# Attention outputs of a hybrid encoder layer copied and added in portions of four query tiles instead of two

## Chip, cores and metric

The kernel runs on one core of a Trainium2 chip. The metric is the device time of one execution in microseconds, as a median over runs; lower is better.

## The reference

One layer of an encoder on a stream of 1024 positions, model width 1024, all in float32: an RMS norm and an input projection; latent attention with 8 heads beside an RWKV-7 recurrence with 8 heads; an output projection; cross-attention to 256 memory tokens; a squared-ReLU MLP with 4096 hidden columns; a final norm. The change lies in the first attention. Cut to that:

```
s = (einsum('bqhd,bkhd->bhqk', qn, k_nope) + einsum('bqhr,bkr->bhqk', qr, k_rope)) * scale
s = where(key_chunk <= q_chunk, s, -inf)          # chunks of 64 positions
p = softmax(s, axis=-1)
o = einsum('bhqk,bkhd->bqhd', p, v)               # 64 value columns per head
o = rms_norm(o, out_norm)                         # per head
```

## The kernel before, in words

Everything is kept transposed, with features on the 128 partitions and the 1024 positions along the free dimension. Each engine has a program of its own, written out by hand, and the engines meet at semaphores. A class `Steps` names every step of a stage on an engine; a wait names the step that it needs, and the list of names (lines 440 to 461) must be in the order in which the engine issues them.

The attention stage runs over 8 heads h and, in each, over 8 query tiles q of 128 positions (here also called slots 0 to 7). A tile sees the keys 0 to 128(q + 1). The steps of a tile are:

- `s` (TensorE, L1071, with a mask product at L1074): the scores of tile q, into PSUM banks 0 to 3.
- `m` (VectorE, `row_max`, L2289): the negative row maximum.
- `e` (ScalarE, `mla_exp`, L1727): the exponential, PSUM to SBUF, with the row sums.
- `t` (TensorE, `mla_turn`, L1085): the probabilities transposed, into banks 4 and 5; `t` (ScalarE, `turned`, L1736) copies them to SBUF.
- `o` (TensorE, `mla_values`, L1102 and L1106): the product with the values, into bank 6. A head has 64 value columns, so the array's halves of 64 columns work on even and odd key tiles: the result of a tile is a sum of two halves of the partitions ("own" and "other").
- `oc` (ScalarE, `keep_other`, L1745) copies the other half from bank 6 to the own partitions of `mO` in SBUF, and then `o` (VectorE, `keep_o`, L2298) adds the own half of bank 6 to it. This is done for two query tiles at once, 256 columns: ScalarE and VectorE issue it in slots 3, 5 and 7 and at the end of the head. The value product of tile q then waits for the addition of the portion before its own (bank 6 is half used, columns 0 to 255 again and again).

TensorE issues in slot q: the scores of q, the turn of q - 1, the values of q - 2, then filler. The filler (`g_fill`, `g_half`, L970) is the input projection of later units, spread over heads 0 to 5 by a plan of quotas; the matmuls of half a unit go to bank 7 and are evicted by VectorE (`evict_half`, L2204 and L2208), in the slot in which the half ends. The next half's first matmul waits for this eviction. In VectorE's queue of a slot stand, in this order, the row maximum, the norm of the pair before in one slot, the addition `keep_o`, the eviction, and the preparation steps below. The query projection of the next head (L1030 to L1034) and the multiplication by the rotary table (`queries`, L2283) come at slot 7.

Heads 6 and 7 have no filler. Beside them go the steps `prep(0, s)` of the recurrence's first pair of heads, placed by `beside_heads(h, q)`: low-rank products (L1140), exponentials with changes of ScalarE's table (L1782 to L1793), elementwise work on VectorE (L2339 to L2402), the 64x64 blocks (L1187, L2387), which SP stores and reads back, and the inverse of their 16x16 blocks by a recurrence on VectorE (L2412, L2415) in slots 5, 6 and 7 and at the end of head 7. Its result is stored in DRAM by SP (L636, L637) and read back in another arrangement (L646); TensorE's first block product of the recurrence's loop (L1277) waits for these reads, and the reads wait also for the last value product.

After two heads GpSimd squares the pair's outputs (`pair_norm`, L779), once the last addition of the pair is done; TensorE sums the squares (L1114), and `o_out` (L2311) scales.

Of the kernel before, what the change touches and what calls it, by code (L numbers as in the profile page):

```python
# [12 lines left out]
ALU = mybir.AluOpType  # L13
AX_X = mybir.AxisListType.X

P = 128
# [148 lines left out]
def build(nc, x_t, mem_t, pos, wall, vecs, con_d, headw, wv_d, lora_d, out_t):  # L165
    with ExitStack() as ctx:
# [245 lines left out]
        for g in range(SLOT_END):  # L412
            n, part, j = part_of(g)
# [27 lines left out]
        for h in range(MLA_HEADS):  # L441
            p, last = h // 2 - 1, h == MLA_HEADS - 1
            for q in range(NW):
                m_pe += [f"s{h}_{q}"] + [f"t{h}_{q - 1}"] * (q >= 1) + [f"o{h}_{q - 2}"] * (q >= 2)
                m_act += [f"e{h}_{q}"] + [f"t{h}_{q - 1}"] * (q >= 1) + [f"oc{h}_{q // 2 - 1}"] * (q in (3, 5, 7))
                m_dve += [f"m{h}_{q}"]
                if p >= 0 and h % 2:
                    m_pe += [f"sp{p}_0", f"sp{p}_1"] * (q == 0)
                    m_dve += [f"ot{p}_0", f"ot{p}_1"] * (q == 1)
                m_dve += [f"o{h}_{q // 2 - 1}"] * (q in (3, 5, 7))  # L450
                if p >= 0 and h % 2 == 0:
                    m_pe += [f"sm{p}"] * (q == 1)
                    m_dve += [f"s2{p}", f"vr{p}"] * (q == 1)
            m_pe += [f"qp{h + 1}"] * (not last) + [f"t{h}_7"] + [f"kp{h + 1}"] * (not last) + [f"o{h}_6", f"o{h}_7"]
            m_pe += [f"vp{h // 2 + 1}"] * (h % 2 == 1 and not last)
            m_act += [f"t{h}_7"] + [f"k{h + 1}"] * (not last) + [f"oc{h}_3"] + [f"v{h // 2 + 1}"] * (h % 2 == 1 and not last)
            m_dve += [f"q{h + 1}"] * (not last) + [f"o{h}_3"]
            m_pool += [f"sq{h // 2}", f"pw{h // 2}"] * (h % 2 == 1)
        p = PAIRS - 1
        m_dve += [f"s2{p}", f"vr{p}", f"ot{p}_0", f"ot{p}_1"]  # L460
# [291 lines left out]
        def _(pool):  # L752
# [20 lines left out]

            def pair_norm(p):

                pool.wait_ge(M_DVE.sem, M_DVE.at(f"o{2 * p + 1}_3", -1))
                if p >= 1:
                    pool.wait_ge(o_stored, 16 * p)
                nc.gpsimd.tensor_tensor(o_stage[:, :], mO[p % 2], mO[p % 2], ALU.mult).then_inc(M_POOL.sem, M_POOL.one(f"sq{p}"))  # L779
                pool.wait_ge(M_DVE.sem, M_DVE.at(f"vr{p}", -1))  # L780
                nc.gpsimd.tensor_tensor(mFac, mSq, con[:, C_NH:C_NH + 16], ALU.pow).then_inc(
                    M_POOL.sem, M_POOL.one(f"pw{p}"))
# [122 lines left out]
        def _(pe):  # L905
# [110 lines left out]
            def m_at(st, name):  # L1016
                pe.wait_ge(st.sem, st.at(name, -1))
# [70 lines left out]
            def mla_values(h, q):  # L1088

                m_at(M_ACT, f"t{h}_{q}")  # L1090
                j, hd = q // 2, h % 2
                if j >= 1:
                    m_at(M_DVE, f"o{h}_{j - 1}")
                elif h >= 1:
                    m_at(M_DVE, f"o{h - 1}_3")
                else:
                    pe.wait_ge(half_free, FILL - 4)
                own, other = (slice(HD * n, HD * n + HD) for n in (hd, 1 - hd))
                at = slice(P * (q % 2), P * (q % 2) + P)
                if q == 0:  # L1100
                    for rows, cols in ((slice(0, HD), own), (slice(HD, P), other)):
                        last = nc.tensor.matmul(PS[cols, 6, at], mV[rows, 0, HD * hd:HD * hd + HD], mPT[0][rows, 0:P],  # L1102
                                                start=True, stop=True)
                else:
                    for k in range(q + 1):
                        last = nc.tensor.matmul(PS[own if k % 2 == 0 else other, 6, at], mV[:, k, HD * hd:HD * hd + HD],  # L1106
                                                mPT[q % 2][:, win(k)], start=(k < 2), stop=(k >= q - 1))
                last.then_inc(M_PE.sem, M_PE.one(f"o{h}_{q}"))
# [542 lines left out]
        def _(act):  # L1651
# [55 lines left out]
            def m_at(st, name):  # L1707
                act.wait_ge(st.sem, st.at(name, -1))
# [28 lines left out]
                    M_ACT.sem, M_ACT.one(f"t{h}_{q}"))  # L1737

            def keep_other(h, j):
                hd, n = h % 2, 2 * P  # L1740
                own, other = (slice(HD * k, HD * k + HD) for k in (hd, 1 - hd))
                m_at(M_PE, f"o{h}_{2 * j + 1}")
                if j == 0 and hd == 0 and h >= 4:
                    m_at(M_DVE, f"ot{h // 2 - 2}_1")
                nc.scalar.copy(mO[h // 2 % 2][own, n * j:n * j + n], PS[other, 6, 0:n]).then_inc(  # L1745
                    M_ACT.sem, M_ACT.one(f"oc{h}_{j}"))
# [172 lines left out]
            for h in range(MLA_HEADS):  # L1919
                if h % 2 == 0 and h >= 4:  # L1920
                    m_at(M_DVE, f"vr{h // 2 - 2}")
                for q in range(NW):
                    mla_exp(h, q)
                    if q >= 1:
                        turned(h, q - 1)
                    if q in (3, 5, 7):
                        keep_other(h, q // 2 - 1)
                    for s in beside_heads(h, q):
                        prep(0, s)
                turned(h, NW - 1)  # L1930
                for s in beside_heads(h, NW):
                    prep(0, s)
                if h < MLA_HEADS - 1:
                    keys(h + 1)
                keep_other(h, 3)
                if h % 2 == 1 and h < MLA_HEADS - 1:
                    values(h // 2 + 1)

# [203 lines left out]
        def _(dve):  # L2142
# [132 lines left out]
            def m(ins, name):  # L2275
                ins.then_inc(M_DVE.sem, M_DVE.one(name))

            def m_at(st, name):
                dve.wait_ge(st.sem, st.at(name, -1))
# [10 lines left out]
                                          negate=True), f"m{h}_{q}")  # L2290

            def keep_o(h, j):
                hd, n = h % 2, 2 * P
                own = slice(HD * hd, HD * hd + HD)
                m_at(M_PE, f"o{h}_{2 * j + 1}")
                m_at(M_ACT, f"oc{h}_{j}")
                o = mO[h // 2 % 2][own, n * j:n * j + n]
                m(nc.vector.tensor_tensor(o, PS[own, 6, 0:n], o, ALU.add), f"o{h}_{j}")  # L2298

            def pair_sums(p):  # L2300
                m_at(M_ACT, f"e{2 * p + 1}_{NW - 1}")
# [212 lines left out]
            for h in range(MLA_HEADS):  # L2514
                for q in range(NW):
                    row_max(h, q)
                    p = h // 2 - 1
                    if h % 2 == 1 and h >= 3 and q == 1:
                        o_out(p, 0)
                        o_out(p, 1)  # L2520
                    if q in (3, 5, 7):
                        keep_o(h, q // 2 - 1)
                    if h % 2 == 0 and h >= 2 and q == 1:
                        pair_sums(p)
                    if q < NW - 1:
                        filled(h, q)
                        for s in beside_heads(h, q):
                            prep(0, s)
# [8 lines left out]
                        evict_half(u, half)  # L2537
                for s in beside_heads(h, NW):
                    prep(0, s)
                keep_o(h, 3)  # L2540
            def attention_end(s):
                if s == 2:
                    pair_sums(PAIRS - 1)
# [435 lines left out]
```

## Time and profile before

| | us |
|---|---|
| median of 3 runs | 1856.16 |
| the runs | 1856.16, 1854.52, 1862.93 |
| the profiled execution | 1852.6 |
| its span, first to last instruction | 1850.5 |

| engine | busy, us | share |
|---|---|---|
| TensorE | 1741.0 | 94% |
| VectorE | 992.4 | 54% |
| ScalarE | 793.5 | 43% |
| GpSimd | 703.9 | 38% |

The mean granted clock of TensorE in the profiled execution is 0.97 of the full level (2.4 GHz). A row of the timeline gives the start in us from the span's beginning, the duration in us, the engine, the line, the operation with output and inputs, and in brackets how long the engine had been idle before it and whose work ended that. PE is TensorE, DVE is VectorE, ACT is ScalarE, POOL is GpSimd; PEld is TensorE's weight load. In rows by stage the order is TensorE, its weight loads, VectorE, ScalarE, GpSimd (busy us and instructions), then the granted clock, DMA share and GB/s.

### The profile page before, as it was taken

The page shows a single profiled execution, that of the slowest core. Times are in us where ns is not written, and L with a number is a line of the kernel's source. Part 1 is how long each engine was busy: PE and PEld are TensorE (multiplying, and loading weights), DVE is VectorE, ACT ScalarE, POOL GpSimd, SP SyncE. Part 2 cuts the span into 40 slices and gives each one's busy share as a digit, 9 for nine tenths or more (in the row PEclk, how much of TensorE's full clock was granted, in tenths as well). Part 3 has the DMA queues.
Part 4 walks back from the last instruction along what each step waited for, and adds up shares of the span by engine and source line. Part 5 has one row for each costly group of instructions (what it writes and reads, how often), then busy time and mean ns, then how long its engine had stood idle before and what let it go on. Part 6 is the DMA issues. An engine that isn't in the chain of part 4 may idle for free.

```text
span 1850.5 us, 29970 instructions
## 1 busy us (share of the span) xinstructions
PE 1741.0 (94%) x11908; PEld 1332.4 (72%) x11908; DVE 992.4 (54%) x1549; ACT 793.5 (43%) x1530; POOL 703.9 (38%) x505
## 2 busy tenths in 40 slices
PE   4999999998788889899999999999999999999996
PEld 3766666655566666668898768778888888888885
DVE  6542232335464655463350262378856775884787
ACT  4313332244233343452130231367566666766762
POOL 1220211011120211232242202297695876968761
PEclk9999999988689999999999999999999999999998
DMA  5101010001111112242211101212112022020202
GB/s 195 53 24 32 23 34 10 21 5 29 41 19 42 20 43 42 88 145 87 88 41 51 34 1 34 76 50 69 50 42 92 23 69 67 26 92 23 69 1 91
DMA packets 81681, 94.35 MB, mean 51 GB/s; under 512 B 53648, under 2 KB 56208, under 8 KB 81552
## 3 DMA queue, kind: packets, MB, share of 16 engines
q1 hardware_dynamic: 81552, 92.56, 15.9%
q8 instruction: 89, 1.46, 0.3%
q14 instruction: 40, 0.33, 0.1%
HBM read 82.57 MB, written 9.98 MB: 50 GB/s over the span
## 4 chain that ended last, share of the span: by engine, by line
PE 84%; DVE 8%; issue 3%; ACT 2%; DMA 1%; POOL 1%; SPq 0%; DVEq 0%; ACTq 0%; POOLq 0%
PE PS L1615 32%; PE PS L922 16%; PE PS L970 8%; PE PS L1071 3%; PE PS L1106 2%; PE PS L1085 2%; PE PS L1140 2%; PE PS L1562 1%; PE PS L1541 1%; PE PS L1433 1%; PE PS L1143 1%; PE PS L1335 1%; PE PS L1418 1%; PE PS L1277 1%; PE PS L1030 1%
## 5 line engine op out<-in xcount | busy, mean ns | idle before, releaser
L1615 PE MATMUL PS<-memr,wsp 128*128 128x512 f32 x1332 | 321.2, 392 | 0.9 <-POOL wsp L883 0.9
L922 PE MATMUL PS<-xn,wsp 128*128 128x512 f32 x1344 | 309.6, 392 | 6.7 <-DVE xn L2158 6.7
L922 PEld LDWEIGHTS PS<-xn,wsp 128*128 128x128 f32 x1344 | 253.5, 189 | 62.0 <-DVE xn L2158 5.0
L1615 PEld LDWEIGHTS PS<-memr,wsp 128*128 128x128 f32 x1332 | 250.6, 188 | 56.0 <-POOL wsp L883 1.3
L762 POOL CAST wsp<-wraw 128x1024 fp32r<-128x1024 f32 x40 | 43.4, 1085 | 472.9 <-PE PS L922 306.5
L1615 PE MATMUL PS<-memr,wraw_r 128*128 128x512 f32 x684 | 167.7, 394 | 5.4 <-DVE memr L2721 3.3
L1615 PEld LDWEIGHTS PS<-memr,wraw_r 128*128 128x128 f32 x684 | 129.0, 189 | 35.2 <-DVE memr L2721 3.7
L970 PE MATMUL PS<-xn,wsp 128*128 128x512 f32 x576 | 146.7, 401 | 3.2 <-DVE proj L2208 3.1
L883 POOL TENSOR_TENSOR wsp<-sa,wsp 128x512 fp32r<-128x512 f32 x86 | 115.1, 1340 | 81.0 <-ACT wsp L2047 80.9
L970 PEld LDWEIGHTS PS<-xn,wsp 128*128 128x128 f32 x576 | 104.4, 188 | 40.1 <-issue 20.2
L2721 DVE TENSOR_TENSOR memr<-PS,memr 128x512 fp32r<-128x512 f32 x168 | 114.6, 682 | 27.4 <-ACT PS L2068 27.4
L1727 ACT ACTIVATE H<-PS,mst 128x128 f32<-128x128 f32 (+3 forms) x64 | 47.5, 741 | 179.8 <-DVE mst L2289 178.2
L1615 PE MATMUL PS<-tmp_r,wsp 128*128 128x512 f32 x444 | 116.9, 397 | 0.0
L2739 DVE TENSOR_TENSOR H<-PS,H 128x512 f32<-128x512 f32 x128 | 86.7, 688 | 46.7 <-PE PS L1615 30.1
L2289 DVE TENSOR_REDUCE mst<-PS 128x1 f32<-128x128 f32 (+3 forms) x64 | 48.2, 754 | 117.3 <-PE PS L1074 117.3
L2063 ACT CAST memr<-sa 128x512 fp32r<-128x512 f32 x96 | 59.2, 617 | 95.1 <-PE PS L1615 78.6
L1615 PEld LDWEIGHTS PS<-tmp_r,wsp 128*128 128x128 f32 x444 | 83.4, 188 | 21.2 <-DVE tmp_r L2721 1.3
L764 POOL TENSOR_TENSOR wsp<-wraw,wsp 128x1024 fp32r<-128x1024 f32 x40 | 96.4, 2410 | 3.2
L867 POOL TENSOR_TENSOR sbx<-sa,sbx 128x512 f32<-128x512 f32 x64 | 85.9, 1342 | 4.7
L883 POOL TENSOR_TENSOR wsp<-sbx,wsp 128x512 fp32r<-128x512 f32 x62 | 82.9, 1341 | 11.1 <-ACT wsp L2047 11.0
L847 POOL TENSOR_TENSOR ssum<-con,rsm 64x256 f32<-64x256 f32 x32 | 27.3, 871 | 139.5 <-DVE ssum L2582 139.5
L1071 PE MATMUL PS<-H 128*128 128x512 f32 (+2 forms) x192 | 77.2, 512 | 0.0
(336 smaller groups left out, 3157.4 us busy)
## 6 DMA issues: line engine op xcount, KB each, us to landing
wraw<-in_weights_dram SPq DMA_DIRECT2D x40, 512.0 KB, 3.6
sa<-in_weights_dram SPq DMA_DIRECT2D x32, 512.0 KB, 4.3
H<-in_x_dram SPq DMA_DIRECT2D x16, 512.0 KB, 6.5
sbx<-in_weights_dram SPq DMA_DIRECT2D x32, 256.0 KB, 2.6
sa<-in_weights_dram SPq DMA_DIRECT2D x32, 256.0 KB, 2.6
H<-in_weights_dram SPq DMA_DIRECT2D x8, 512.0 KB, 6.7
out_dram<-sbx SPq DMA_DIRECT2D x16, 256.0 KB, 2.1
a_dram<-H SPq DMA_DIRECT2D x16, 128.0 KB, 2.5
```

The source lines that it names most:

```text
L764: nc.gpsimd.tensor_tensor(wsp[:, k, :, 1, :], raw, wsp[:, k, :, 0, :].bitcast(F32), ALU.subtract).then_inc(w_split, 1)
L867: nc.gpsimd.tensor_tensor(out, a, b, op).then_inc(W_SUM.sem, W_SUM.one(name))
L883: nc.gpsimd.tensor_tensor(w[:, 1, :], w_source(g), w[:, 0, :].bitcast(F32), ALU.subtract).then_inc(mw_rest, 1)
L922: last = nc.tensor.matmul(PS[:, 2 * k + half, :], wsp[:, k, kt, a, :], src[:, at, b, HALF * half:HALF * half + HALF], start=(i == 0 and (a ...
L970: last = nc.tensor.matmul(PS[:, bank, :], wsp[:, u % 2, kt, a, :], xn[:, kt, b, HALF * half:HALF * half + HALF], start=(kt == 0 and (a, b) ...
L1071: nc.tensor.matmul(PS[:, b + part, 0:n], mQ[:, win(q)], mK[:, HALF * part:HALF * part + n], start=True, stop=(part < q // 4))
L1615: last = nc.tensor.matmul(PS[:, g % PS_BANKS, :], w[:, a, win(k)], x[:, b, :], start=(k == 0 and (a, b) == (0, 0)), stop=(k == ROWS - 1 an ...
L1727: nc.scalar.activation(mP[q % 2][:, 0:n], two(2 * (q % 2))[:, 0:n], ACT.Exp, bias=mNeg[hd][:, q:q + 1], accum_out=mSum[h // 2 % 2][:, c:c ...
L2063: nc.scalar.copy(x_split_of(d)[:, 0, :], x_source(d)).then_inc(mx_head, 1)
L2289: m(nc.vector.tensor_reduce(mNeg[h % 2][:, q:q + 1], two(2 * (q % 2))[:, 0:P * (q + 1)], AX_X, ALU.max, negate=True), f"m{h}_{q}")
L2721: nc.vector.tensor_tensor(x[:, 1, :], PS[:, PS_BANKS + d % 2, :], x[:, 0, :].bitcast(F32), ALU.subtract).then_inc(mx_rest, 1)
L2739: out(nc.vector.tensor_tensor(tile, a, b, ALU.add), f"{kind}{part}_{v}")
```

## The change

The portion copied from and added out of bank 6 becomes four query tiles, 512 columns, the whole bank, instead of two tiles and half the bank. ScalarE and VectorE issue the pair in slot 5 and at the end of the head only. The value product of tile 4 waits for the first portion's addition, that of tile 0 for the second portion of the head before. The additions' steps are renamed from `o` to `a`. Nothing else is edited.

```diff
@@ lists of steps
-                m_act += [f"e{h}_{q}"] + [f"t{h}_{q - 1}"] * (q >= 1) + [f"oc{h}_{q // 2 - 1}"] * (q in (3, 5, 7))
+                m_act += [f"e{h}_{q}"] + [f"t{h}_{q - 1}"] * (q >= 1) + [f"oc{h}_0"] * (q == 5)
...
-                m_dve += [f"o{h}_{q // 2 - 1}"] * (q in (3, 5, 7))
+                m_dve += [f"a{h}_0"] * (q == 5)
...
@@ pair_norm, GpSimd
-                pool.wait_ge(M_DVE.sem, M_DVE.at(f"o{2 * p + 1}_3", -1))
+                pool.wait_ge(M_DVE.sem, M_DVE.at(f"a{2 * p + 1}_1", -1))
@@ mla_values, TensorE
-                j, hd = q // 2, h % 2
+                j, hd = q // 4, h % 2
                 if j >= 1:
-                    m_at(M_DVE, f"o{h}_{j - 1}")
+                    m_at(M_DVE, f"a{h}_{j - 1}")
                 elif h >= 1:
-                    m_at(M_DVE, f"o{h - 1}_3")
+                    m_at(M_DVE, f"a{h - 1}_1")
...
-                at = slice(P * (q % 2), P * (q % 2) + P)
+                at = slice(P * (q % 4), P * (q % 4) + P)
@@ keep_other, ScalarE
-                hd, n = h % 2, 2 * P
+                hd, n = h % 2, 4 * P
...
-                m_at(M_PE, f"o{h}_{2 * j + 1}")
+                m_at(M_PE, f"o{h}_{4 * j + 3}")
@@ the loop over slots, ScalarE
-                    if q in (3, 5, 7):
-                        keep_other(h, q // 2 - 1)
+                    if q == 5:
+                        keep_other(h, 0)
...
-                keep_other(h, 3)
+                keep_other(h, 1)
@@ keep_o, VectorE
-                hd, n = h % 2, 2 * P
+                hd, n = h % 2, 4 * P
...
-                m_at(M_PE, f"o{h}_{2 * j + 1}")
+                m_at(M_PE, f"o{h}_{4 * j + 3}")
                 m_at(M_ACT, f"oc{h}_{j}")
                 o = mO[h // 2 % 2][own, n * j:n * j + n]
-                m(nc.vector.tensor_tensor(o, PS[own, 6, 0:n], o, ALU.add), f"o{h}_{j}")
+                m(nc.vector.tensor_tensor(o, PS[own, 6, 0:n], o, ALU.add), f"a{h}_{j}")
@@ the loop over slots, VectorE
-                    if q in (3, 5, 7):
-                        keep_o(h, q // 2 - 1)
+                    if q == 5:
+                        keep_o(h, 0)
...
-                keep_o(h, 3)
+                keep_o(h, 1)
```

## Rows read from the trace of the kernel before

**Rows 1.** The page: busy time, share of the span and instructions.

```profile
PE 1741.0 (94%) x11908; PEld 1332.4 (72%) x11908; DVE 992.4 (54%) x1549; ACT 793.5 (43%) x1530; POOL 703.9 (38%) x505
```

**Rows 2.** Busy time by stretch, columns as told above.

```profile
120.00:390.00 270.00, 266.78 (x1505) 179.02 (x1505) 83.72 (x124) 82.72 (x179) 36.83 (x20) 1.00 0.06 21
390.00:474.00 84.00, 73.07 (x473) 41.34 (x469) 41.08 (x80) 40.45 (x77) 11.42 (x5) 0.86 0.08 19
399.00:412.00 13.00, 11.28 (x21) 3.64 (x21) 3.87 (x4) 6.42 (x9) 1.77 (x1) 0.50 0.00 0
478.00:511.00 33.00, 28.80 (x265) 20.31 (x266) 8.15 (x19) 8.03 (x17) 4.37 (x3) 0.50 0.20 50
```

**Rows 3.** Groups by shape: busy us, mean ns, idle before and releaser.

```profile
L2298 DVE TENSOR_TENSOR H<-PS,H 64x256 f32<-64x256 f32 x16 | 6.8, 422 | 44.9 <-ACT H L1745 44.9
L2298 DVE TENSOR_TENSOR mO_odd<-PS,mO_odd 64x256 f32<-64x256 f32 x16 | 6.7, 422 | 32.1 <-ACT mO_odd L1745 32.1
L1745 ACT COPY H<-PS 64x256 f32<-64x256 f32 x16 | 5.9, 366 | 9.4 <-PE PS L1106 9.2
```

**Rows 4.** A copy of 64x512 (duration min/median/max in ns), an addition of 128x512.

```profile
L1712 ACT COPY H<-PS x8: 578/580/581, 114.5 to 432.4; 64x512 f32<-64x512 f32 x8
...
L2739 DVE TENSOR_TENSOR H<-PS,H 128x512 f32<-128x512 f32 x128 | 86.7, 688 | 46.7 <-PE PS L1615 30.1 <-ACT con L2083 8.2 <-issue 7.2
```

**Rows 5.** Timeline, head 2, slots 5 and 6.

```profile
232.23 0.37 ACT L1745 COPY mO_odd<-PS 64x256 f32<-64x256 f32 x1
232.70 0.42 DVE L2298 TENSOR_TENSOR mO_odd<-PS,mO_odd 64x256 f32<-64x256 f32 x1 [2.10 <-ACT mO_odd L1745]
...
233.81 0.75 DVE L2208 SCALAR_TENSOR_TENSOR proj<-PS,vec,proj 128x511 f32<-128x511 f32 x1
...
234.70 1.62 PE L970 MATMUL PS<-xn,wsp 128*128 128x512 f32 x6 [0.15 <-DVE proj L2208]
```

**Rows 6.** Timeline, head 1, slots 3 and 4.

```profile
175.48 0.43 DVE L2298 TENSOR_TENSOR H<-PS,H 64x256 f32<-64x256 f32 x1 [1.67 <-ACT H L1745]
...
177.62 1.61 PE L970 MATMUL PS<-xn,wsp 128*128 128x512 f32 x6 [0.42 <-DVE proj L2208]
```

**Rows 7.** Timeline, head 6: slot 3, and its end.

```profile
413.34 0.37 ACT L1745 COPY mO_odd<-PS 64x256 f32<-64x256 f32 x1
...
436.13 0.41 DVE L2298 TENSOR_TENSOR mO_odd<-PS,mO_odd 64x256 f32<-64x256 f32 x1
```

**Rows 8.** Timeline, head 7, slot 3.

```profile
450.29 1.12 PE L1143 MATMUL PS<-proj,con 128*128 128x512 f32 x2
...
451.30 0.43 DVE L2298 TENSOR_TENSOR mO_odd<-PS,mO_odd 64x256 f32<-64x256 f32 x1 [1.67 <-ACT mO_odd L1745]
...
452.30 0.69 DVE L2402 TENSOR_TENSOR proj<-PS,proj 128x512 f32<-128x512 f32 x1
```

**Rows 9.** Timeline, head 7, VectorE in slots 5 and 7.

```profile
461.26 0.43 DVE L2298 TENSOR_TENSOR mO_odd<-PS,mO_odd 64x256 f32<-64x256 f32 x1 [2.10 <-ACT mO_odd L1745]
...
466.49 1.22 DVE L2289 TENSOR_REDUCE mst<-PS 128x1 f32<-128x1024 f32 x1
...
470.23 0.43 DVE L2298 TENSOR_TENSOR mO_odd<-PS,mO_odd 64x256 f32<-64x256 f32 x1 [2.52 <-ACT mO_odd L1745]
470.69 0.23 DVE L2412 TENSOR_TENSOR sc_s<-sc_s 128x63 f32<-128x63 f32 x1
```

**Rows 10.** Timeline, from the last value product and the recurrence's result to the first block product.

```profile
473.19 0.36 ACT L1745 COPY mO_odd<-PS 64x256 f32<-64x256 f32 x1 [1.19 <-PE PS L1106]
...
474.05 0.38 DVE L2418 COPY sc_s<-sc_s 128x256 f32<-128x256 f32 x1
...
478.95 1.28 SPq L646 DMA_DIRECT2D H<-x_dram  x2
...
479.42 0.69 PE L1260 MATMUL PS<-sc_s,sc_w 64*64 64x64 f32 x8 [0.18 <-ACT sc_s L1829]
...
484.13 1.12 PE L1277 MATMUL PS<-H 64*64 64x64 f32 x16 [4.02 <-DMA H<-xt_dram]
```

More of the change, by code:

```diff
@@ L455, in build @@
             m_pe += [f"vp{h // 2 + 1}"] * (h % 2 == 1 and not last)
-            m_act += [f"t{h}_7"] + [f"k{h + 1}"] * (not last) + [f"oc{h}_3"] + [f"v{h // 2 + 1}"] * (h % 2 == 1 and not last)
-            m_dve += [f"q{h + 1}"] * (not last) + [f"o{h}_3"]
+            m_act += [f"t{h}_7"] + [f"k{h + 1}"] * (not last) + [f"oc{h}_1"] + [f"v{h // 2 + 1}"] * (h % 2 == 1 and not last)
+            m_dve += [f"q{h + 1}"] * (not last) + [f"a{h}_1"]
             m_pool += [f"sq{h // 2}", f"pw{h // 2}"] * (h % 2 == 1)
```

## Prediction, made before the changed kernel was run

> **What bounds the kernel now.** The first view is the page: TensorE is busy for 94% of the span, no other engine for more than 54% [rows 1], so a step counts only where TensorE waits for it. The second view is busy time by stage. In the heads whose slots are filled with projection matmuls (120 to 390 us, nearly all of heads 0 to 5) TensorE is busy 266.78 of 270 us; in heads 6 and 7 (390 to 474 us), which have no such filler, 73.07 of 84 us, at a mean clock of 0.86 [rows 2]. So heads 0 to 5 can give back 3.2 us at most, whatever is taken from ScalarE and VectorE, and the question is heads 6 and 7. The third view, groups of instructions by shape, shows the edited pair: 32 copies of 64x256 at 366 ns on ScalarE and 32 additions at 422 ns on VectorE, and 44.9 + 32.1 = 77 us in which VectorE stood idle before an addition until the copy was done [rows 3]. That number is large because VectorE works strictly in order; it costs time only where the work queued behind the addition is itself waited for. The rest of the reading is a hunt for those places.
>
> **What changes.** 16 pairs of copy and addition in place of 32, each twice as wide, at query slot 5 and at the head's end instead of slots 3, 5, 7 and the end. TensorE's matmuls and their order stay. Each value product still waits once, for the addition that frees bank 6: o4 waits for the first portion, o0 of the next head for the second; the waits of o2 and o6 fall on work long done.
>
> **Prices.** A 64x512 copy out of PSUM stands in the trace: 580 ns. A 64x512 addition does not; its bounds are the 64x256 one (422 ns) and two of those (844 ns), and the addition over 128x512, as many elements per partition, takes 688 ns [rows 3, 4]. I take 690 ns, the nearest in shape. Per pair that is +0.21 us on ScalarE and +0.27 us on VectorE where a pair stays, and all of it away where one goes. Over the kernel ScalarE saves 32 x 0.366 - 16 x 0.580 = 2.4 us and VectorE 32 x 0.422 - 16 x 0.690 = 2.5 us, on engines that are about half idle.
>
> The Trainium skill (VectorE: DVE Perf Modes, the section on the TRN2 errata) says that each instruction pays a fixed cost once and advises tiles of 512 elements or more. Read as advice on the whole time it would credit the change with those 4.9 us; the stage view says that nearly all of them lie beside a busy TensorE.
>
> **Heads 0 to 5.** Two places matter, both evictions of the projection, which stand behind the addition in VectorE's queue and free the bank that the next filler wants. In head 2, slot 5, copy (232.23), addition (232.70) and eviction (ends 234.56) come in a row, and the filler at 234.70 already waits 0.15 us for it [rows 5]. The wider pair delays this by 0.21 + 0.27 = 0.48 us. Head 5 repeats the pattern (filler at 374.51): +0.96 us together. The opposite is found in heads 1 and 4, slot 3: there the pair disappears, the eviction can start when its matmuls end, about a microsecond earlier, and the filler's waits of 0.42 and 0.29 us go (head 1 is shown) [rows 6]: -0.71 us. Sum +0.25 us; ends +0.96 and -0.71. SP's and POOL's queues wait on these evictions only through the weight tiles, and POOL is idle for most of this stretch; hiding the rest is TensorE's own filler. If that cover were gone these heads would look like 6 and 7.
>
> **Head 6.** ScalarE is the chain from 412 to 421 us (two table loads, exponentials, copies). The copy at 413.34 goes: -0.39 us with its gap. At slot 5 the wider copy and addition stand between t4's copy and the next row maximum: +0.48 us. Net +0.1 us. At the head's end the addition at 436.13 sits in an unbroken run of VectorE work that TensorE waits for: +0.27 us [rows 7]. The addition removed at slot 7 was followed by a wait for the query projection, so it gives nothing.
>
> **Head 7, slot 3.** After the row maximum (ends 449.6) VectorE waited 1.67 us for the copy, added (451.30), wrote two small memsets and only then did the multiplication at 452.30 whose operand TensorE had finished at 451.42; the next score matmuls are behind that multiplication [rows 8]. Without the pair the memsets run early and it starts at 451.5: -0.79 us.
>
> **Head 7, slot 5.** Copy and addition stay, wider, with the block-inverse recurrence queued behind them: +0.48 us [rows 9].
>
> **Head 7, slot 7.** This is the largest term. The row maximum ends at 467.71. The addition then waits for the copy, which stands behind an exponential and a turned copy on ScalarE: 2.52 us idle, done at 470.66, and only at 470.69 does VectorE go on with the recurrence [rows 9], whose result (474.4) is stored, read back and waited for by TensorE until 484.13 [rows 10]. Without this portion the recurrence goes on at 467.71: -2.98 us. Is another wait hidden beneath? The reads of the stored blocks also wait for the last value product, done at 473.1 [rows 10], and for the stores, which would now land near 476; they then start at 476, still later. TensorE's work before the reads ends near 480.1 with the copies that follow it [rows 10]; the wider last addition, since VectorE now waits for its copy, moves this by -0.3 us, to 479.8, against 481.2 for the data. So 1.4 us of room remain and all 2.98 us pass. The store of the last pair and POOL's squaring behind the last addition start about 0.3 us earlier too, and the squares are first used after the reads.
>
> **Sum.** +0.25 + 0.1 + 0.27 - 0.79 + 0.48 - 2.98 = -2.67 us. By the ends of the addition's price (422 or 844 ns) the five wide additions in these chains change it by about -1.3 or +0.8 us. Against the profiled execution (1852.6 us, of it a span of 1850.5) that gives 1849.9 us. The median of the three runs stands 3.6 us above that execution; so I forecast 1856.2 - 2.7 = 1853.5 us. The three runs spread over 8.4 us, three times the effect, and about 0.5% (9 us) is what a measurement of this kernel can tell from no change.
>
> **Rivals.**
> First, nothing is gained: the early recurrence meets something the trace of before cannot show, such as the stores running slower beside other traffic, or the recurrence's interleaving with the row maxima shifting so that TensorE waits for those instead. It needs 1.4 us or more of new delay at 476 to 484 us to eat half the gain. Against it speaks that the DMA queue is otherwise empty there. Time: 1856.2 us.
>
> Second, TensorE's clock. It is granted at half level (1.2 GHz) from 478 to 511 us, TensorE busy 28.8 of 33 us [rows 2], right after a stretch of thin work and a 4 us idle gap before 484.13 [rows 10]. The change shortens that gap to about 1.4 us. If the full level survived it, up to half of 28.8 = 14.4 us would go; part of it is held by other engines, so I take 8: 1845.5 us. Against: the clock had fallen by 478, before the gap, in a stretch whose matmuls the change moves by only 0.3 to 0.6 us. The Trainium skill (TensorE: Matmul & The Clock Gate, on oscillation) says that idle gaps throttle the array and sustained work releases it; by that rule the shorter gap speaks for this rival, while the trace puts the fall ahead of the gap.
>
> Third, the other sign: one more half-level stretch in heads 6 and 7. There TensorE is idle in places, and the clock has already gone to half at 399 to 412 us with 11.28 us busy [rows 2]. If the delays at slot 5 thin out its work enough that the clock falls once more for as long, the loss is up to half of 11.28 = 5.6 us; with the gain, +2.9: 1859.1 us. It decides from a fall longer than about 6 us. The place to see it is 460 to 475 us, where the trace now grants the full clock. Slower by over 0.5% needs two such stretches.
>
> That the change does not do what it says is excluded by the code: each engine's list of steps and its waits are changed alike.
>
> **Chances.** Forecast 0.67; nothing gained 0.12; clock better 0.08; clock worse 0.13. The range 1846.0 to 1860.0 takes in the forecast with the addition's bounds, nothing gained, most of the clock cases and the spread of the runs. Faster by over 0.5% (under 1846.9) needs the clock case and a good draw: 0.05. Slower by over 0.5% (above 1865.4) needs two worse stretches or a disturbed set: 0.04. Within 0.5%: 0.91.
>
> **What would show each step.** The copy 16 times at 580 ns and the addition 16 times near 690; VectorE's idle before it falling from 77 us to about half; the fillers of heads 2 and 5 after slot 5 waiting 0.6 to 0.8 us, those of heads 1 and 4 not at all; no gap of 2.5 us on VectorE after the last row maximum of head 7; the first block matmul about 2.7 us earlier relative to the start. I am wrong if that matmul moves by less than 1 us or if heads 0 to 5 end over 1 us later.

## The result, and the profile after

| | before | after |
|---|---|---|
| median of 11 executions each, in alternation | 1856.16 us | 1846.1 us |
| ratio after/before, 95% interval | | 0.9938, 0.9915 to 0.996 |
| profiled execution | 1852.6 us | 1841.3 us |
| its span, mean granted clock | 1850.5 us, 0.970 | 1839.5 us, 0.972 |

The kernel became faster by 0.6% (0.4 to 0.85%), 10 us between the medians and 11.5 us by the ratio, where 2.7 us were forecast. One execution of the 11 after took 2455 us at a mean clock of 0.648, and in the runs further down one of e1 took 9312 us and one of e7 1865.3 us; the ratios leave these out.

**The edited pair** came out as priced. The groups by shape of the kernel after (busy us, mean ns, idle before and releaser):

```profile
L2298 DVE TENSOR_TENSOR H<-PS,H 64x512 f32<-64x512 f32 x8 | 5.5, 688 | 29.8 <-ACT H L1745 29.8
L2298 DVE TENSOR_TENSOR mO_odd<-PS,mO_odd 64x512 f32<-64x512 f32 x8 | 5.5, 688 | 20.7 <-ACT mO_odd L1745 20.7
L1745 ACT COPY H<-PS 64x512 f32<-64x512 f32 x8 | 4.6, 580 | 9.3 <-PE PS L1106 9.2
```

Against [rows 3], half the instructions, 688 ns (690 assumed) and 580 ns each. VectorE's idle time before them fell from 77 to 50.5 us, to two thirds where about half was expected. That fall of 26.5 us is not what the kernel gained: TensorE, as before, sets the time.

**The stages** (busy time by stretch; columns as in [rows 2]):

```profile
120.00:390.00 270.00, 266.61 (x1511) 179.12 (x1510) 82.03 (x112) 80.69 (x167) 36.82 (x20) 1.00 0.07 21
390.00:474.00 84.00, 73.45 (x442) 42.26 (x440) 40.15 (x77) 39.48 (x72) 11.41 (x5) 0.82 0.10 20
399.00:412.00 13.00, 10.63 (x17) 3.35 (x17) 3.45 (x3) 6.58 (x10) 1.58 (x1) 0.50 0.00 0
478.00:511.00 33.00, 31.32 (x480) 22.99 (x480) 17.82 (x39) 16.19 (x37) 6.26 (x5) 0.95 0.18 45
```

Heads 0 to 5 are as they were. The last row is the news. Before, 33 us at clock 0.50 held 265 matmuls [rows 2]; now they hold 480, at 0.95. TensorE reads as busy in both. A busy share says nothing of the pace: the count of matmuls and the clock column do.

The same work, cut at the same two instructions (from the first block product to the first state product of the recurrence), in the kernel after and then, in the second fence, before:

```profile
481.60:498.40 16.80, 16.41 (x260) 11.24 (x256) 8.32 (x15) 6.64 (x11) 4.49 (x3) 1.00 0.17 45
```

```profile
484.10:512.60 28.50, 28.47 (x250) 19.52 (x250) 7.94 (x15) 6.46 (x10) 4.37 (x3) 0.51 0.13 34
```

By the starts of those two instructions it is 28.51 - 16.74 = 11.8 us, as much as the whole difference of the two profiled executions (11.3 us). The first block product comes 2.5 us earlier than before, and the time after the first state product is 3.2 us longer (1839.5 - 498.4 against 1850.5 - 512.6). That last part was not followed further: two profiled executions of the unchanged kernel differ by 6.4 us (1852.6 and, in the first run below, 1859.0). The 2.5 us are one draw too: 0.9 of them stand already at the first key projection of the attention (113.42 against 112.55 us), and a second stretch at half level, near 440 us, which the prediction did not name, lasted about 10 us before and 7 us after.

**The place.** The timeline of the kernel after, head 7 slot 7 to the first block product:

```profile
466.03 1.22 DVE L2289 TENSOR_REDUCE mst<-PS 128x1 f32<-128x1024 f32 x1
...
467.16 0.22 DVE L2412 TENSOR_TENSOR sc_s<-sc_s 128x63 f32<-128x63 f32 x1
...
470.51 0.38 DVE L2418 COPY sc_s<-sc_s 128x256 f32<-128x256 f32 x1
...
475.43 1.28 SPq L646 DMA_DIRECT2D H<-x_dram  x2
...
481.36 0.45 PE L1260 MATMUL PS<-sc_s,sc_w 64*64 64x64 f32 x8 [0.18 <-ACT sc_s L1829]
...
481.64 0.63 PE L1277 MATMUL PS<-H 64*64 64x64 f32 x16
```

The 2.52 us stall of [rows 9] is gone, the recurrence goes on right behind the row maximum, and the read of the stored blocks is issued at 475.43 instead of 478.95 [rows 10]. TensorE no longer waits before the first block product: 4.02 us had been forecast to become 1.4, and became none. Why none? TensorE's own work ran later than forecast. Busy time by stretch, after:

```profile
466.00:470.00 4.00, 2.57 (x22) 2.06 (x23) 3.62 (x14) 2.01 (x4) 0.00 (x0) 0.69 0.01 4
470.00:474.00 4.00, 4.00 (x33) 3.67 (x33) 0.79 (x4) 1.01 (x1) 0.00 (x0) 0.50 0.48 57
474.00:478.00 4.00, 1.84 (x40) 1.19 (x37) 1.76 (x3) 0.58 (x1) 1.76 (x1) 0.93 0.27 51
478.00:482.00 4.00, 3.62 (x39) 3.25 (x41) 2.21 (x6) 1.75 (x8) 0.14 (x1) 0.60 0.85 192
482.00:486.00 4.00, 3.84 (x74) 3.55 (x70) 1.48 (x5) 0.12 (x1) 0.00 (x0) 1.00 0.59 163
```

and before:

```profile
470.00:474.00 4.00, 3.57 (x54) 2.75 (x53) 3.29 (x15) 1.50 (x3) 0.00 (x0) 1.00 0.00 0
474.00:478.00 4.00, 1.68 (x25) 1.47 (x26) 3.13 (x6) 0.31 (x2) 1.89 (x1) 0.95 0.56 66
478.00:482.00 4.00, 1.94 (x19) 1.33 (x18) 0.95 (x5) 1.56 (x7) 0.00 (x0) 0.50 0.29 66
482.00:486.00 4.00, 1.87 (x30) 1.75 (x32) 0.58 (x2) 0.00 (x0) 0.00 (x0) 0.50 0.98 202
```

After, TensorE's clock fell to half already in 466 to 474 us, came back, fell once more, and was full from 482 on. Before, it fell at about 478 and stayed at half through the wait and the step behind it. The early fall stretched TensorE's own work so far that the data were there when it asked. The Trainium skill (TensorE: Matmul & The Clock Gate, on what is actually happening and on oscillation) has activity release the throttle and idle gaps bring it back. These two traces fit the second half: thin work and gaps stand ahead of each of these falls. The first half does not hold for the step before, busy 28.47 of 28.5 us and not raised. That step is made of small products in the main, but not of those alone: 9.6 us of it are products of 512 columns (L1140 and L1143).

### The profile page after: what moved, and what is told of

Its sections match the earlier page's. It is cut to its first block, busy times and chain, and to the rows that moved or that the text cites. A ratio compares the mean times of both kernels' runs of the same rounds, so it can differ in the third digit from the quotient of the medians.

```text
span 1839.5 us, 29922 instructions
## 1 busy us (share of the span) xinstructions
PE 1735.1 (94%) x11908; PEld 1330.3 (72%) x11908; DVE 992.0 (54%) x1533; ACT 791.1 (43%) x1514; POOL 703.9 (38%) x505
## 4 chain that ended last, share of the span: by engine, by line
PE 84%; DVE 8%; issue 2%; ACT 2%; DMA 1%; POOL 1%; SPq 1%; DVEq 0%; ACTq 0%; POOLq 0%
PE PS L1615 32%; PE PS L922 16%; PE PS L970 8%; PE PS L1071 3%; PE PS L1106 2%; PE PS L1085 2%; PE PS L1562 2%; PE PS L1140 1%; PE PS L1541 1%; PE PS L1433 1%; PE PS L1143 1%; PE PS L1335 1%; PE PS L1418 1%; PE PS L1030 1%; PE PS L1366 1%
```

## The experiments

Each kernel ran in alternation with the kernel before, whose median was 1859.0 us beside e1 to e4, 1856.7 beside e5 to e8 and 1857.3 beside e9 to e12; these three sets ran on three chips. Here is what they gave; the texts on record and what follows from each come after. "Wait" is TensorE's idle time ahead of the first block product in the profiled execution, "step" the time from it to the first state product, with its clock; the last column counts executions under 1848 us, which is below every one of the 115 of the kernel before in all sets (lowest 1850.3). It is no exact measure of the level in the step: the profiled execution of e10 had the full level there and took 1849.5 us.

| label | median us | ratio to before (95%) | wait | step (clock) | under 1848 |
|---|---|---|---|---|---|
| before, first set | 1856.2 | | 4.0 | 28.5 (0.51) | 0 of 11 |
| after | 1846.1 | 0.9938 (0.9915-0.996) | none | 16.8 (1.00) | 7 of 11 |
| e1_before_again | 1857.9 | 0.9988 (0.9965-1.0011) | 4.8 | 28.8 (0.51) | 0 of 12 |
| e2_after_again | 1846.1 | 0.9936 (0.991-0.9963) | none | 16.8 (1.00) | 7 of 12 |
| e3_late_four | 1858.9 | 0.9985 (0.9954-1.0015) | 2.2 | 28.5 (0.52) | 2 of 12 |
| e4_stall_back | 1854.8 | 0.9974 (0.9948-1.0001) | 1.1 | 29.0 (0.51) | 0 of 12 |
| e5_before_gap | 1849.0 | 0.9973 (0.995-0.9996) | filled, 0.5 left | 16.8 (1.00) | 5 of 12 |
| e6_after_busy | 1851.6 | 0.9968 (0.9954-0.9983) | 2.3 | 28.6 (0.52) | 2 of 12 |
| e7_head7_four | 1844.2 | 0.9926 (0.9904-0.9949) | 2.3 | 28.5 (0.52) | 7 of 11 |
| e8_early_four | 1857.4 | 1.001 (0.9988-1.0033) | 2.6 | 28.6 (0.52) | 0 of 12 |
| e9_heads05_four | 1857.0 | 1.0005 (0.9984-1.0026) | 3.2 | 28.9 (0.51) | 0 of 12 |
| e10_head7_gap | 1852.7 | 0.9979 (0.9957-1.0) | filled | 16.8 (1.00) | 4 of 12 |
| e11_head7_gap_scores | 1845.5 | 0.9938 (0.9913-0.9963) | filled | 23.9 (0.64) | 9 of 12 |
| e12_head7_four_again | 1846.2 | 0.9961 (0.9934-0.9987) | none | 16.7 (1.00) | 7 of 12 |

**Both kernels again**, unchanged, as a measure of chance.

> The kernel before, once more, for a second profile of it. Theory A (the earlier block data keep TensorE's clock up in the recurrence's loop): the ratio to the kernel before is 1.000 within 0.2%, and in this profile too the clock is at half level from about 478 us to past 505 us. Theory B (where the clock falls and rises is chance in each execution, and the two profiles compared were two draws): the stretch at half level after 478 us differs by 10 us or more from that of the first profile.

> The changed kernel, once more. Theory A: ratio about 0.994 again, and the clock is at the full level from about 482 us on in this profile as well. Theory B: about 0.9985 (the 2.7 us of the sum) with a clock stretch of any length.

The kernel before came out at 1857.9 us with the same half-level step behind a wait of 4.81 us; the kernel after at the same median as the first time. So 0.6% is the change's and no draw of one set. One part of the first expectation missed: the level was not at half from 478 us on but full until about 485, and fell within the wait (483.0 to 487.8 us):

```profile
478.00:482.00 4.00, 1.93 (x28) 1.53 (x28) 3.12 (x7) 0.81 (x5) 1.89 (x1) 1.00 0.56 66
482.00:486.00 4.00, 0.85 (x16) 0.57 (x16) 0.53 (x2) 0.98 (x5) 0.00 (x0) 0.92 0.41 94
```

So in one and the same program the level falls ahead of the wait or within it, and the step is slow either way. In e2 the first block product came at 487.21 us, only 0.6 us earlier than in e1 and 5.6 us later than in the first profile of the same kernel. Its half-level stretch near 440 us lasted 17 us, where those of before and e1 lasted 10 and that of after 7:

```profile
448.00:452.00 4.00, 3.54 (x21) 1.85 (x22) 1.05 (x3) 0.00 (x0) 0.00 (x0) 0.50 0.15 31
452.00:456.00 4.00, 3.22 (x10) 0.98 (x8) 1.51 (x4) 1.15 (x3) 0.00 (x0) 0.50 0.62 98
```

Yet TensorE had no wait and the step took 16.8 us, at full level from 487 us on and not, as theory A had it, from 482. That the block product comes early is not what makes the step quick.

**Other portions.** The bounds of the portions were made a function of the head, which all loops, waits and step lists read; the kernels differ in its one line. Its versions, one under the other:

```
return ((0, 2), (2, 4), (4, 8))                                            # e3_late_four
return ((0, 4), (4, 6), (6, 8))                                            # e8_early_four
return ((0, 4), (4, 8)) if h == 7 else ((0, 2), (2, 4), (4, 6), (6, 8))    # e7, e12
return ((0, 4), (4, 8)) if h < 6 else ((0, 2), (2, 4), (4, 6), (6, 8))     # e9
```

The first, e3, keeps two-tile portions early and has no addition in slot 7, so the stall of [rows 9] is gone in it.

> Portions of 2, 2 and 4 tiles: the pair of slot 7 goes, those of slots 3 and 5 stay as before. Theory A: this carries nearly the whole gain, since the recurrence's result is stored about 3 us earlier: the first block product starts near 481 us, the clock is up from about 482 us, ratio 0.993 to 0.995. Theory B: the first block product is early by 3 us but the ratio is 0.998.

The wait shrank to 2.19 us, and the step ran at half level; 0.9985 is no difference that can be told. Theory A had the block product near 481 us and a ratio of 0.993 to 0.995, and missed with both; theory B's ratio came, its block product 3 us early did not:

```profile
485.52 0.68 PE L1295 MATMUL PS<-H 64*64 64x64 f32 x16 [2.19 <-DMA H<-xt_dram]
```

This speaks against the reading that the removed stall alone buys 10 us. In this profile the level was full through the wait and fell within the first microsecond of the step.

**The stall put back.** The change as it is, but VectorE waits in head 7, slot 7, for ScalarE's turned copy, where the removed addition had held it.

```diff
                     if q == 5:
                         keep_o(h, 0)
+                    if h == MLA_HEADS - 1 and q == NW - 1:
+                        m_at(M_ACT, f"t{h}_{q - 1}")
```

> The changed kernel with one wait added: in head 7, slot 7, VectorE waits after the row maximum for ScalarE's turned copy of tile 6, about 2.3 us. Theory A: the data come 2.3 us later than in the changed kernel, the clock stays at half level after 484 us as before, and most of the 10 us are lost again: ratio 0.998 to 1.000. Theory B: 2.3 us slower than the changed kernel and no more.

The stall returned at 2.06 us, TensorE waited 1.11 us, and the median is 8.7 us above that of the change:

```profile
468.67 1.22 DVE L2289 TENSOR_REDUCE mst<-PS 128x1 f32<-128x1024 f32 x1
...
471.96 0.23 DVE L2412 TENSOR_TENSOR sc_s<-sc_s 128x63 f32<-128x63 f32 x1 [2.06 <-ACT H L1736]
...
485.67 1.12 PE L1277 MATMUL PS<-H 64*64 64x64 f32 x16 [1.11 <-DMA H<-xt_dram]
```

Two microseconds of stall cost over eight, and none of the twelve executions came under 1848 us. The level fell at about 480 us, ahead of the wait, as it had after (478 us); after, without a wait, it rose at 481, and here, behind 1.1 us of wait, it stayed at half through the step. So the stall is needed for the slower outcome here, though, by e3, its absence is not enough for the quicker one.

**The wait filled.** Two full 128x512 products whose results nobody reads, between TensorE's last wait ahead of the block products and the first of these, in the kernel before.

```diff
+            def keep_busy(n):
+                r_at(P_DVE, "bv1_0")
+                for _ in range(n):
+                    nc.tensor.matmul(PS[:, 7, :], ident, con[:, 0:HALF], start=True, stop=True)
...
             pe.wait_ge(rp_dve, RP_SET)
+            keep_busy(2)
```

> The kernel before, portions of two, with two 128x512 products of constants into the free bank 7 where TensorE waits 4 us for the block data. Nothing is computed from them. Theory A (it is TensorE's wait ahead of the loop that keeps the clock at half level to 513 us): the clock is up within a few us of 484 us, and 8 us or more are gained with the portions unchanged, ratio 0.994 to 0.997. Theory B (chance, or the portions themselves): ratio 1.000 and the half level lasts to past 505 us.

```profile
479.60 3.78 PE L1441 MATMUL PS<-con 128*128 128x512 f32 x4
...
483.88 0.70 PE L1277 MATMUL PS<-H 64*64 64x64 f32 x16 [0.50 <-DMA H<-xt_dram]
```

Here nothing of the portions was changed and the stored blocks are as late as ever. The level fell at about 477 us, as in the first profile of before, and came back at 484.0, as the first block product started; there it had stayed down past 511 us. The step ran at full level, 16.8 us, in the profiled execution, the median is 7.7 us below that of the kernel before beside it, and 5 of 12 executions came under 1848 us, where the kernel before never does. The ratio, 0.9973, is just short of what theory A asked for. So it is the idle wait on TensorE, and not the data's lateness, that goes with the slow step in this pair. It is the cleanest of the experiments, and it also shows that filling the wait is no sure cure. The filling is itself work of 512 columns; that other work, or none but an absent wait, does as well is shown by the kernel after.

**More filling.** The change with such products elsewhere in thin places: two in slot 7 of head 7, one before the last turn, one behind each of the first two score steps, and none in the wait.

> The changed kernel with such products in five places where TensorE waits: two in slot 7 of head 7, one before its last turn, one behind each of the first two score steps of the loop. Theory A: the clock stays at the full level through 466 to 482 us and the low executions of the changed kernel vanish; ratio 0.990 to 0.993. Theory B: each product costs up to its 0.9 us, ratio 0.994 to 0.996 and the same spread.

A half-level step in the profiled execution, behind a wait of 2.26 us, only 2 of 12 under 1848 us, and 0.9968, slower than either theory's ratio. The level itself was full from 466 to 482 us, as theory A had it, and through the wait; it fell within the first microsecond of the step. So a level held up to the wait was no help here. The products' own time is in the 1851.6 us.

**Which heads.** Next came the change in head 7 alone (e7), in heads 0 to 5 alone (e9), and the early four (e8), which keeps an addition in slot 7.

> Portions of four in head 7 alone, two elsewhere. Theory A: the whole direct gain of 3 us (slots 3 and 7 of head 7) plus the clock, so ratio 0.993 to 0.995 with heads 0 to 6 unchanged. Theory B: ratio 0.998.

> Portions of 4, 2 and 2 tiles: the pair of slot 3 goes, those of slot 7 and the end stay as before. Theory A: the direct gain is under 1 us, the data come as late as before and the clock stays low: ratio 0.999 to 1.000. Theory B (the whole effect hangs on how the work falls, from anywhere): any ratio from 0.994 to 1.003.

> Portions of four in heads 0 to 5 only, two in heads 6 and 7. By the sum heads 0 to 5 lose about 0.25 us and everything behind them stays: ratio 1.000 within 0.2%, clock at half level from 478 to past 505 us in nearly every execution. If the wider portions there mattered, the ratio would lie outside 0.998 to 1.002.

Head 7 alone gives as much as the whole change (0.9926, and 0.9961 the second time), heads 0 to 5 nothing (1.0005), and the early four, whose addition in slot 7 still waits for its copy, nothing (1.001):

```profile
475.83 0.43 DVE L2318 TENSOR_TENSOR mO_odd<-PS,mO_odd 64x256 f32<-64x256 f32 x1 [2.53 <-ACT mO_odd L1764]
```

The profiled execution of e7 is one of the four of eleven that took longer (1853.2 us). It shows a full level ahead of the wait and a half-level step behind it:

```profile
478.00:482.00 4.00, 1.71 (x24) 1.24 (x22) 1.56 (x5) 1.79 (x8) 0.00 (x0) 1.00 0.74 168
...
482.43 0.78 PE L1295 MATMUL PS<-H 64*64 64x64 f32 x16 [2.30 <-DMA H<-xt_dram]
...
482.40:510.90 28.50, 28.41 (x252) 19.27 (x252) 7.94 (x15) 6.47 (x10) 4.38 (x3) 0.52 0.11 31
```

**The same kernel once more** (e12), with e10 and e11, which add products in the wait, and in the wait and behind each score step, to head 7 alone.

> Portions of four in head 7 alone, once more, for a second profile and more executions. Ratio 0.992 to 0.995 again. Theory A: where the profiled execution is a fast one (under 1845 us), the first state product follows the first block product by about 17 us; where it is a slow one, by about 28 us.

> Portions of four in head 7 alone, and two 128x512 products of constants into the free bank 7 where TensorE waits 2.3 us for the block data. Theory A (TensorE's wait there decides the clock of the loop's first step): nearly all executions have the full level from the first block product on, so the first state product follows it by 17 and not by 28 us; ratio 0.990 to 0.992. Rival (the portions' gain is used up, the products only cost): ratio 0.993 to 0.995 and the spread stays.

> As the kernel before this one, with one more such product behind each of the first two score steps, where TensorE waits 1.6 and 0.8 us. If more filling keeps the clock up more often: ratio 0.988 to 0.991. If these products delay the block product instead (the 0.8 us wait is shorter than the product): 1 us slower than the kernel with the two products alone.

This time the profile caught one of the quick executions of that kernel:

```profile
483.22 0.63 PE L1295 MATMUL PS<-H 64*64 64x64 f32 x16
...
483.20:499.90 16.70, 16.31 (x258) 11.20 (x252) 8.32 (x15) 6.64 (x11) 4.49 (x3) 1.00 0.16 45
```

e7 and e12 are one program. With a wait of 2.30 us the step took 28.5 us, with none 16.7: 11.8 us, and the twelve executions of e12 lie in two groups, 7 between 1843 and 1848 us (mean clock 0.971 to 0.974) and 5 between 1855 and 1861 us (0.963 to 0.966), about 12 us apart. The program does not decide which of the two an execution takes, and the share differs from kernel to kernel. That the two groups are the two outcomes of this step is inferred from the distance and the clock; one execution of e12 was profiled.

e11 has the most executions in the quick group (9 of 12) and no better median, and its profile shows the step at full level for about five microseconds only, though TensorE had not waited ahead of it:

```profile
485.70:489.70 4.00, 3.84 (x71) 3.62 (x72) 1.37 (x4) 0.00 (x0) 0.00 (x0) 1.00 0.36 121
489.70:507.00 17.30, 17.30 (x168) 10.45 (x164) 5.00 (x9) 5.19 (x10) 4.04 (x3) 0.54 0.01 2
```

e10 went the other way than hoped, 4 of 12 and a median of 1852.7 us, slower than either theory had it. Filling the wait lets the level be full in the profiles (e5, e10 and, for a while, e11), while over all executions it helps the kernel before (0 of 115 to 5 of 12) and does nothing that can be told for head 7 alone (7 of 11 and 7 of 12, against 4 and 9 of 12).

**What the profiles say together.** Of 14 (before, after and the twelve), eight have an unfilled wait, of 1.1 to 4.8 us: the step took 28.5 to 29.0 us in all eight. In the six without one it began at full level, and took 16.7 to 16.8 us in five.

The wait is not the whole of it. In e3, e6, e7 and e8 the level was still full when the block product started behind a wait of 2.2 to 2.6 us, and fell within the first microsecond of the step. In e11, whose wait was filled and whose level had been full since 477 us, it fell at about 491. All five quick steps came the other way: the level had fallen less than ten microseconds before the block product and rose within a microsecond of its start, or in e10 2.5 us before it. There are five more profiles in which it had fallen in those ten microseconds, all with a wait (before, e1, e4, e9, and e8, where it had come back at 487.2 us, 2.9 us ahead of the block product, and was lost again), and in all of them the step ran at half level. So in these ten the wait tells the two outcomes apart. Where the level had not fallen in that time (e3, e6, e7, e11), no profile shows it held, with a wait or without; whether the removal of the wait is worth anything there is not shown.

**The rest, with the clock taken out.** Each execution comes with its mean granted clock. A line through the executions of one kernel, time against clock, read at 0.967, gives 1857.4 us for the kernel before beside e1 to e4, one execution at a clock of 0.921 left out (1856.6 and 1857.5 in the two later sets), 1855.1 and 1853.2 for the change (e2), 1853.9 and 1854.0 for head 7 alone, 1854.4 for the late four, 1855.4 for the early four, 1856.6 for heads 0 to 5. At one clock the change is worth 2.3 us (4.2 in e2), head 7 alone 2.7 and 3.5, the late four about 3, heads 0 to 5 about 1 or nothing. These are fits through a dozen points each, good to perhaps a microsecond or two. They would suit a direct part of the size of the forecast sum, 2.7 us, in head 7, but they don't show it: the same line gives 1854.9 us for e4, 2.5 us under the kernel before, though its stall is back.

The timelines say a little more. From head 6's first low-rank product (L1140) to the first block product it is 90.9 us in before and 91.8 in e1, 89.0 in after and 92.8 in e2, 87.7 and 88.4 with head 7 alone (e7, e12), and 93.2 in e9. Where the half-level stretch near 440 us is equally long, 10 us, head 7 alone has the block product 2.5 to 4.1 us earlier (before and e1 against e7 and e12); where it lasts 17 us, the change has it 0.4 us earlier (e2 against e9).

## Why the prediction was wrong, by its own steps

The sum of the direct effects has its size confirmed only within a microsecond or two; the step that failed is the weighing of the second rival, which put the clock behind the wait at 0.08 and at nothing in the sum.

- **Prices**: copy 580 ns, addition 688 ns (690 taken). Right.
- **Heads 0 to 5**, +0.25 us: from the first key projection to the first low-rank product behind head 5 it is 279.8 us before and 280.0 after. The fillers of heads 2 and 5 wait 0.60 and 0.73 us (0.63 and 0.77 by the sum); those of heads 1 and 4 don't wait. Head 2, from the timeline after:

```profile
230.94 0.58 ACT L1745 COPY mO_odd<-PS 64x512 f32<-64x512 f32 x1
231.62 0.68 DVE L2298 TENSOR_TENSOR mO_odd<-PS,mO_odd 64x512 f32<-64x512 f32 x1 [2.32 <-ACT mO_odd L1745]
...
233.00 0.75 DVE L2208 SCALAR_TENSOR_TENSOR proj<-PS,vec,proj 128x511 f32<-128x511 f32 x1
...
233.90 3.23 PE L970 MATMUL PS<-xn,wsp 128*128 128x512 f32 x13 [0.60 <-DVE proj L2208]
```

- **Slot 5.** A cost that the sum lacked: in two places the value product of tile 4 now waits for the wider addition, 0.55 us in head 6 (423.76 us) and 0.23 us in head 7:

```profile
461.38 0.84 PE L1106 MATMUL PS<-H,tmp 128*64 128x128 f32 x10 [0.23 <-DVE mO_odd L2298]
```

The prediction named this wait and put no price on it.

- **Head 6**, +0.1 and +0.27 us: no run measures these two terms by themselves, and the half-level stretch near 440 us lies behind them.
- **Head 7, slot 3**, -0.79 us: the small memsets now follow the row maximum at once, and the multiplication starts 2.74 us after the row maximum's start (448.63 to 451.37) instead of 3.36 (448.94 to 452.30): -0.62 us.
- **Head 7, slot 7**, -2.98 us: the gap of 2.52 us is gone, and the recurrence's result is written 3.5 us earlier (470.51 against 474.05), the first block product starts 2.5 us earlier. The stall's own price was right. The sign set for being wrong, a block product less than 1 us earlier, did not come with the first profile (2.5 us), but would have with the second pair (0.6 us, e2 against e1), in which the stretch near 440 us hid it. What was not right: of the 4.02 us wait 1.4 us were to be left. In the executions with a wait it was 2.2 and 2.3 us (e3, e7), in those where TensorE's clock fell in slot 7 there was none (after, e2, e12).
- **The second rival** had the mechanism right, the clock behind a shorter gap, and 0.08 of the chance. Its price was also short: 8 us where the step measures 11.8 us, since of the 14.4 us that it allowed I let other engines hold 6.4. The words that failed are "against: the clock had fallen by 478, before the gap". The fall ahead of the gap is a fact of the trace before, and it was taken for a cause that the change doesn't reach. The runs show in its place that the fall's place decides nothing: the level fell at 477 to 478 us in before and e5, and also in after, for the second time there, in e1 only at 485, and in e3, e6 and e7 only behind the wait; and that in these profiles a level that has fallen comes back where TensorE does not wait (at 481 us after, at 484 in e5) and stays down where it waits (before, e1, e4, e9). The question ought to have been what would have raised it again, not when it fell. The rule of the Trainium skill (TensorE: Matmul & The Clock Gate, on oscillation) that idle gaps throttle the array, quoted in the prediction as speaking for this rival, pointed the right way and was set aside for the wrong reason.
- **The other rivals** did not decide: no delay at 476 to 484 us ate the gain, and the half-level stretch at 399 to 412 us is unchanged. A further fall did come in slot 7 (0.69 and 0.50 in 466 to 474 us), as the third rival had it; it took from TensorE some microseconds that it would otherwise have spent waiting.

**What stays open.** What decides, in one execution, where between 466 and 491 us the level falls, and how long the half-level stretch near 440 us lasts (7, 10 or 17 us). And why the late four, with the stall gone, a direct gain near the change's by the fit, and the same wait of 2.2 us in its profile as e7, comes under 1848 us in 2 of 12 executions where head 7 alone does in 14 of 23: they differ in the pairs of slot 3, which shift the work of head 7 by a microsecond or less, and in heads 0 to 6; they also ran on different chips, and no run here separates that. That the wait keeps a fallen level down rests on e5, where it alone was filled, on e4, where it alone was put back, and on ten of the 14 profiles; the shares of executions are counts of twelve and carry no finer distinction than none, some and most.

No version tried clearly beats the change: head 7 alone (0.9926 and 0.9961) and its filled version e11 (0.9938) have intervals that overlap those of the change (0.9938 and 0.9936).

## What to carry to other kernels

Behind a place where the clock column reads one half although TensorE is busy, look at the wait ahead of it: if it can be shortened or filled, the gain can be the difference of the two levels over all the work behind it, here 11.8 us from a wait of 4. Here it came in a share of the executions only, so it takes many executions to see, and filling the wait brought it in 5 of 12 at best for the kernel before and added nothing that can be told to head 7 alone. Count matmuls per microsecond, not busy time. When a pair of small instructions is merged on an engine that works in order, look at what stands in its queue behind the pair: of the 26.5 us of idle time that this change removed, the 2.5 us ahead of a store and a read are the part that mattered: with 2.06 us of them put back, 8.7 of the 10 us were lost. They were needed and not enough, as e3 shows.

## What the runs showed of the hardware that had not been expected

- A step of mostly small products kept TensorE busy for 28.47 of 28.5 us without the granted clock leaving half level. The same step begun at full level kept it in five of ten profiles: e3, e6, e7 and e8 lost it within a microsecond, e11 after about five.
- One program can have two outcomes about 12 us apart on one core, and the mean granted clock of the execution tells which it was (e12: 0.963 to 0.966 or 0.971 to 0.974).
- One program can also have a stretch at half level of very different length in the same place: near 440 us, 7 us in after and 17 us in e2.
- An early fall of the clock can go with a shorter time. Of one and the same program, the execution whose level was full through slot 7 waited 2.30 us and took 1853.2 us (e7), and the one whose level was 0.50 in 470 to 474 us did not wait and took 1844.5 (e12). It is no rule: in e4 the level fell at 470 too, and TensorE waited 1.11 us.
- An addition from PSUM over 64 partitions of 512 elements takes what one over 128 partitions takes, 688 ns [rows 3, 4]. This one was as priced. The Trainium skill (VectorE: DVE Perf Modes, the section on the TRN2 errata) has a fixed cost per instruction, and the pairs of 422 ns at 256 elements and 688 ns at 512 agree with it: twice the elements cost 1.63 times the time.
